# Two fused transformer layers on one Trainium2 core: the second feature projection by seven quadrant products, and another order for the end of the pass before it

## The reference

```python
xn = _rms_norm(x, norm_g[l]) * (1.0 + sc_x) + sh_x
fx_in, fx_gate, qx, kx, vx, nx_gate = _split_proj(xn @ w_in[l])
qx = _rms_norm(_heads(qx), q_norm_g[l])      # heads of 64
kx = _rms_norm(_heads(kx), k_norm_g[l])
```

## Time and profile before

| | us |
|---|---|
| median of 3 runs | 3401.26 (3400.95 to 3413.02) |
| the profiled execution, its own time | 3402.36 |
| its span (first to last instruction) | 3400.6 |
| second token pass, with the start of the feature pass | about 1845 to 2153 |
| second feature pass after its barrier | 2153.3 to 2693 |

### The profile page before, as it was taken

One profiled execution on the slowest core, in us unless ns is written; L12 is line 12 of the kernel. 1 busy time (PEld: TensorE's weight loads), 2 busy tenths in 40 slices (PEclk: granted clock), 3 DMA queues, 4 the chain that ended last, 5 costly groups with the idle time before them and its releaser, 6 DMA issues. The chain is left out here.

```text
span 3400.6 us, 39668 instructions
## 1 busy us (share of the span) xinstructions
PE 3111.9 (92%) x14503; PEld 2445.2 (72%) x14503; DVE 1514.0 (45%) x2504; ACT 941.8 (28%) x1520; POOL 795.5 (23%) x842
## 2 busy tenths in 40 slices
PE   3799999999988999775998999899999898999899
PEld 2588887888876666553897877677888675666687
DVE  6643333042306666386455222476000145777633
ACT  4422212110112334342222234322011133555400
POOL 5322222111112222265342222011111041000111
PEclk7899999999998999778898999999999998999999
DMA  7534335122243341314102666323211235776475
GB/s 272 184 97 116 102 101 180 61 77 75 75 127 87 90 105 55 90 47 97 43 26 82 200 185 208 109 112 123 74 74 74 99 102 134 155 158 142 112 199 148
DMA packets 325559, 390.82 MB, mean 115 GB/s; under 512 B 93879, under 2 KB 260264, under 8 KB 310696
## 3 DMA queue, kind: packets, MB, share of 16 engines
q1 hardware_dynamic: 320692, 387.11, 39.9%
q10 hardware_dynamic: 4704, 1.59, 0.2%
HBM read 256.77 MB, written 135.79 MB: 115 GB/s over the span
## 5 line engine op out<-in xcount | busy, mean ns | idle before, releaser
L691 PE MATMUL f_psum_out<-f_x_high,f_w_high 128*128 128x512 f32 (+1 forms) x1472 | 573.5, 390 | 18.8 <-DVE f_x_low L668 8.1
L691 PE MATMUL f_psum_out<-f_x_low,f_w_high 128*128 128x512 f32 (+1 forms) x1472 | 569.0, 387 | 0.0
L691 PE MATMUL f_psum_out<-f_x_high,f_w_low 128*128 128x512 f32 (+1 forms) x1472 | 568.6, 386 | 0.0
L691 PEld LDWEIGHTS f_psum_out<-f_x_high,f_w_high 128*128 128x128 f32 x1472 | 279.1, 190 | 77.9 <-issue 15.0
L691 PEld LDWEIGHTS f_psum_out<-f_x_low,f_w_high 128*128 128x128 f32 x1472 | 278.9, 189 | 56.5 <-issue 1.7
L691 PEld LDWEIGHTS f_psum_out<-f_x_high,f_w_low 128*128 128x128 f32 x1472 | 278.9, 189 | 55.5
L1351 PE MATMUL nbr_psum_o<-nbr_probT,nbr_v 128*128 128x512 f32 (+3 forms) x576 | 235.8, 490 | 0.0
L683 POOL CAST f_w_high<-f_w 128x1024 fp32r<-128x1024 f32 x41 | 42.6, 1040 | 747.8 <-PE f_psum_out L691 550.5
L532 PE MATMUL p_psum_proj<-p_w_high,p_h_high 128*128 128x512 f32 x512 | 207.5, 405 | 7.4 <-issue 4.0
L532 PE MATMUL p_psum_proj<-p_w_low,p_h_high 128*128 128x512 f32 x512 | 202.1, 395 | 0.0
L532 PE MATMUL p_psum_proj<-p_w_high,p_h_low 128*128 128x512 f32 x512 | 202.1, 395 | 0.0
(11 more groups left out here) (541 smaller groups left out, 6134.0 us busy)
## 6 DMA issues: line engine op xcount, KB each, us to landing
f_w<-in_w_fm SPq DMA_DIRECT2D x45, 512.0 KB, 5.7
side_ada_w<-in_w_ada_rows SPq DMA_DIRECT2D x24, 512.0 KB, 5.7
scratch_qkmT<-p_qkT_out SPq DMA_DIRECT2D x32, 384.0 KB, 4.6
scratch_z1T<-f_out SPq DMA_DIRECT2D x10, 1024.0 KB, 4.8
p_z<-scratch_z1T SPq DMA_DIRECT2D x16, 640.0 KB, 6.6
p_xt<-in_x SPq DMA_DIRECT2D x16, 512.0 KB, 3.9
p_staging<-in_w_tok SPq DMA_DIRECT2D x8, 1024.0 KB, 8.0
scratch_hT<-p_h_slot SPq DMA_DIRECT2D x16, 512.0 KB, 3.3
```

The lines of the kernel that those rows point to most:

```text
L691: last = nc.tensor.matmul(self.p_out[b][:, n * BANK + lo:n * BANK + hi], self.w_parts[b][w_part][:, k, :], self.x_parts[x_part][:, n, k, l ...
```

## The change

The product `W @ X` (output features by tokens) is cut into quadrants: W by pairs of output blocks and halves of the 1024 input features, X by halves of the input features and by even and odd tiles of 128 tokens. With sums of quadrants, seven quadrant products and some additions replace eight quadrant products. Everything below is one diff.

- `xn` is stored as `x2q`: the four quadrants of X (one of even or odd tiles each) and with them three sums and differences and a fourth, so 7 operands of [128, 4, 1024]; `combine` forms T1 to T4, by POOL for pairs 0 to 6 and by DVE for pair 7.
- The feature pass runs 24 items: 2 halves of the tokens by 12 pairs of blocks. An item is 7 products of 12 instructions each (4 slices, 3 parts), each into its own PSUM bank of six; DVE merges them. POOL adds weight quadrants and takes the rests, ACT rounds them, once for each item. The 7 input operands of a half stand in SBUF and are loaded again for the second half in item 11.
- The head norms take sums of 2 rows (2-column ones), which go to DRAM and come back spread over 128 partitions for root and reciprocal, go to DRAM again and come back broadcast.
- Results stand in three sets of rows (`SETS`), the third in the memory of the Fourier weights, which are loaded in item 20 instead of at the start.
- q and k items alternate with v and Fourier-input items (`F2_ORDER`). Loops of the pass are unrolled.
- In the token pass `before_pair` and `before_last` hold other work (`begin_next`, `go_on`), the last `turn_x` of tile 14 moves into the products of tile 15, and the last slot is filled by DVE.

```diff
+class QuadrantPass:
+    A11, A12, A22, S1, S2, S3, S4 = range(7)
+    B11, B21, B22, T1, T2, T3, T4 = range(7)
+    PRODUCTS = ((A11, B11), (S2, T2), (A12, B21), (S3, T3), (A22, T4), (S1, T1), (S4, B22))
+    N, HK, BANKS = 7, KB // 2, 6
+    def load_w(self, sp, n):
+        if n >= 2:
+            sp.wait_ge(self.a_ready, self.N * (n - 1))
+        sp.dma_start(<w[n % 2], two blocks, 1 MB>).then_inc(self.w_in[n % 2], 16)
+    def load_x(self, sp, half, i):
+        if half:
+            sp.wait_ge(self.prod_ready, self.N * (half * self.per_half - 1) + i + 1)
+        sp.dma_start(<x[i], 1 MB>).then_inc(self.x_in[i], 16)
+    def round_x(self, act, half, i):
+        act.wait_ge(self.x_in[i], 16 * (half + 1))
+        self.nc.scalar.activation(self.x[i][1][:], self.x[i][0][:], ACT.Copy).then_inc(self.x_rounded, 1)
+    def rest_of_x(self, eng, ops, half, i):
+        eng.wait_ge(self.x_rounded, self.N * half + i + 1)
+        ops.tensor_tensor(low, raw, high, ALU.subtract).then_inc(self.x_ready[i], 1)
+    def add_weights(self, pool, n):
+        pool.wait_ge(self.w_in[n % 2], 16 * (n // 2 + 1))
+        nc.gpsimd.tensor_tensor(s1, a21, a22, ALU.add)
+        nc.gpsimd.tensor_tensor(s3, a11, a21, ALU.subtract)
+        pool.drain()
+        nc.gpsimd.tensor_tensor(s2, s1, a11, ALU.subtract)
+        pool.drain()
+        nc.gpsimd.tensor_tensor(s4, a12, s2, ALU.subtract).then_inc(self.sums_ready, 1)
+    def round_w(self, act, n, i):        # waits prod_ready of item n-1, product i, and w_in or sums_ready
+    def rest_of_w(self, pool, n, i):     # waits a_rounded; tensor_tensor, 128x512
+    def product(self, pe, n, i):
+        pe.wait_ge(self.a_ready, self.N * n + i + 1)
+        if n % self.per_half == 0:
+            pe.wait_ge(self.x_ready[i], n // self.per_half + 1)
+        if self.N * n + i >= self.BANKS:
+            pe.wait_ge(self.prod_free, self.N * n + i + 1 - self.BANKS)
+        <12 matmuls of 128x512 into one bank>
 # tile_pass_2
+    def combine(eng, ops, j):
+        eng.wait_ge(combined_stored, 16 * (j + 1))
+        <4 tensor_tensor of 128x512, drains between>.then_inc(combined_ready, 1)
     def move(j, b):
         wait_apart(sp, x_filled, i + 1, taken)
-        sp.dma_start(cols_of(d["x2T"], i), slot[b][:])
+        <b == 0: slot[0] whole; b == 1: half of slot[1]>
+    def move_combined(j): <waits combined_ready, stores 1 MB>
     SP tile:
+        if b == 1 and not second and not last:
+            move_combined(j - 1)
         sp.wait_ge(x1_ready[b], j + 1)
-    next_weights (before_pair): fp.load(sp, d["w_fm2"], 0, b) for b in range(2)
-    begin_next (before_last):
-        sp.wait_ge(slices_used, 1)
-        fp.load_input(sp, d["x2T"], 0, 2)
-        sp.wait_ge(x1_ready[1], PAIRS)
-        fp.load_input(sp, d["x2T"], 2, 3)
+    begin_next (before_pair): fp.load_w(sp, 0); fp.load_x(sp, 0, 0)
+    go_on (before_last):
+        sp.wait_ge(mix_ready[1], PAIRS); sp.wait_ge(o_ready, NT - 1)
+        fp.load_x(sp, 0, 1)
+        move_combined(PAIRS - 2)
+        sp.wait_ge(slices_used, 1)
+        fp.load_x(sp, 0, 2); fp.load_x(sp, 0, 3)
+        sp.wait_ge(slices_used, 2)
+        fp.load_x(sp, 0, 4); fp.load_x(sp, 0, 5)
-    tiles(sp, tile, next_weights, begin_next)
+    tiles(sp, tile, begin_next, go_on)
+    sp.wait_ge(o_ready, NT); fp.load_x(sp, 0, 6); fp.load_w(sp, 1)
     move(PAIRS - 1, 1)
+    move_combined(PAIRS - 1)
 # PE after tile 15
-    fp.project_piece(nc, pe, 0, 0); turn_x(NT - 1); fp.project_piece(nc, pe, 0, 1)
-    pe.wait_ge(x_filled, NT); <pieces 0, 1 of block 1, piece 2 of both>
+    for i in range(fp.BANKS):
+        if i == 4:
+            pe.wait_ge(x_filled, NT)
+        fp.product(pe, 0, i)
+        if i == 1:
+            turn_x(NT - 1)
 # ACT
     fill: act.wait_ge(slot_stored[b], 16 * (j + 1))
+          act.wait_ge(combined_stored, 16 * (j + 1))
+    begin_next (before_pair): fp.round_x(act, 0, 0); fp.round_w(act, 0, i) for i in range(7)
+    go_on (before_last): fp.round_x(act, 0, 1); fill(PAIRS - 1, 0); fp.round_x(act, 0, 2); fp.round_x(act, 0, 3)
+    after the tiles: fp.round_x(act, 0, i) for i in range(4, 7)
 # POOL
+    tile, b == 0: wait_apart(pool, x_filled, 2 * j, taken); combine(pool, nc.gpsimd, j - 1)
+    begin_next: fp.add_weights(pool, 0); fp.rest_of_w(pool, 0, i) for i in range(3)
+    go_on: fp.rest_of_w(pool, 0, i) for i in range(3, 7);   at the end: fp.rest_of_x(pool, nc.gpsimd, 0, 5)
 # DVE
-    tiles(dve, tile, before_last=lambda: fp.rest_of_input(nc, dve, 0, 1))
+    begin_next (before_pair): fp.rest_of_x(dve, nc.vector, 0, 0)
+    go_on (before_last): fp.rest_of_x(dve, nc.vector, 0, 1);   in tile 15: rest_of_x 2
+    after the tiles: rest_of_x 3; <8 tensor_scalar fill slot[1]>; rest_of_x 4; combine(dve, nc.vector, PAIRS - 1); rest_of_x 6
+F2_ORDER = (0, 4, 1, 5, 2, 6, 3, 7, 8, 9, 10, 11)
 # feature_pass_2, one item n on each engine (kind: qk, v, in, gate)
+ SP:   load_w(n + 2); if n-1 is qk: spread_sums(n-1); store(n-1) if qk or v; n == 11: load_x(1, i) for 7 i;
+       n == 20: Fourier weights; store(n) if in or gate
+       spread_sums: rows -> rms_in (DRAM) -> spread [128,16] -> (root, reciprocal) -> rms_out (DRAM) -> work, broadcast to 64 partitions twice
+ PE:   product(n, i); after product 0 and 1 the sums of a qk item n-1 (two fp32 products each, ones[:, 0:P:HD]);
+       after product 1 and 3 the eight transposes each of a v item n-1
+ POOL: add_weights(n); rest_of_w(n, i) for 7 i
+ ACT:  round_w(n+1, i); empty sums or transposes of n-1; at i == 5: roots(n-1) and Square or Silu of n, b = 1; at the end b = 0
+ DVE:  merge(n, i): 8 operations of 128x512 an item, each frees a bank (prod_free); at i == 5 two reciprocals of 128x16;
+       after merge(n, 6): norm(n-1, 1), norm(n-1, 0), which wait for rms_in; n == 11: rest_of_x(1, i-3) after merges 3 to 6, then the last three
-    of_fourier loads at the start of the pass, Fori loops over pairs, RECIPROCAL of 128x2048
```

More of the change, by code:

```diff
@@ L2108, in _ @@
                 sp.sem_inc(slot_stored[b], 16)
+            sp.sem_inc(combined_stored, 16)
             load_x(0, 0)
@@ L2175, in tile @@
                     turn_y(j + 1, b)
-                if not first:
+                if not first and not (last and b == 1):
                     turn_x(2 * j + b - 1, first=second)
@@ L2212, in tile, with go_on @@
                     high(j + 1, b)
-                if not first:
+                if not first and not (last and b == 1):
                     fill(j + b - 1, 1 - b)
             def begin_next():
-                for b in range(2):
-                    fp.round_first_weights(nc, act, b)
-                fp.round_input(nc, act, 0, 2)
+                fp.round_x(act, 0, 0)
+                for i in range(fp.N):
+                    fp.round_w(act, 0, i)
+            def go_on():
+                fp.round_x(act, 0, 1)
+                fill(PAIRS - 1, 0)
+                fp.round_x(act, 0, 2)
+                fp.round_x(act, 0, 3)
             for k in range(MB):
@@ L2227, in _ @@
                 nc.scalar.activation(w_parts[0][:, k], staging[k % BUFFERS][:], ACT.Copy).then_inc(w_high_ready, 1)
-            tiles(act, tile, before_last=begin_next)
-            fill(PAIRS - 1, 1)
-            fp.round_input(nc, act, 2)
+            tiles(act, tile, begin_next, go_on)
+            for i in range(4, fp.N):
+                fp.round_x(act, 0, i)
         @block.gpsimd
@@ L2244, in tile, with go_on @@
                     low(j + 1, b)
+                if b == 0 and not first:
+                    wait_apart(pool, x_filled, 2 * j, taken)
+                    combine(pool, nc.gpsimd, j - 1)
             def begin_next():
-                for b in range(2):
-                    fp.rest_of_first_weights(nc, pool, b)
+                fp.add_weights(pool, 0)
+                for i in range(LOWS_FIRST):
+                    fp.rest_of_w(pool, 0, i)
+            def go_on():
+                for i in range(LOWS_FIRST, fp.N):
+                    fp.rest_of_w(pool, 0, i)
             low(0, 0, slice(LOW_FIRST, MB))
             low(0, 1)
-            tiles(pool, tile, before_last=begin_next)
+            tiles(pool, tile, begin_next, go_on)
+            fp.rest_of_x(pool, nc.gpsimd, 0, 5)
         @block.vector
@@ new lines, in _ @@
+            dve.wait_ge(slot_stored[1], 16 * PAIRS)
+            dve.wait_ge(combined_stored, 16 * PAIRS)
+            for k in range(KB):
+                nc.vector.tensor_scalar(slot[1][:, k, :], p_x[:, k, :], g.scale_x[:, k:k + 1], g.shift_x[:, k:k + 1], ALU.mult, ALU.add)
+            dve.drain().then_inc(x_filled, 1)
+            dve.wait_ge(x_filled, NT)
+            fp.rest_of_x(dve, nc.vector, 0, 4)
+            combine(dve, nc.vector, PAIRS - 1)
+            fp.rest_of_x(dve, nc.vector, 0, 6)
@@ L2375, in turn_v @@
-            def turn_v(j, b):
-                pe.wait_ge(vT_ready[b], j - FIRST_V + 1)
-                for n in range(NT):
```

(14 more changed lines are left out.)

497 lines of the change are left out of this document (344 added, 153 removed).

## The result

The changed kernel takes 3364.57 us (median of 4 runs, 3361.53 to 3367.08), the kernel before 3402.35 (4 runs, 3400.95 to 3413.02). The ratio is 0.9882, 95% interval 0.986 to 0.9904: faster by 1.2%. Forecast were 3343 us and a range of 3328 to 3372. The sign and the range held, the gain was 38 us where 59 were forecast, and the time lies 8.6 us outside the likeliest case's own range (3333 to 3356). The profiled execution took 3361.53 us with a span of 3359.8, so it stands against the 3344.4 of the sum: 17.1 us more.

A forecast was written before the change was run, and what follows sets the result against it. The feature pass was taken as bound by PE, the seam by loads, rounding and rests. From 3402.4, 61 us saved and 3 added gave 3344.4 for the profiled execution, 3343 as median; range 3328 to 3372.

The forecast's parts named there:

- 8, product (1, 0): New seam before the feature pass: tile 15 starts 9.2 us later, barrier 4.5 us earlier, item 1's first product at 2155.7.
- boundaries: Unrolled code and 161 product boundaries in the feature pass: 0 to 0.05 us each, 3 us added.
- part 7: Token pass: changed stores and the fill's wait cost +1 us over seven pairs, bounds -5 and +20.
- part 9: End of feature pass: shorter last silu and store take away about 1.2 of the 6.8 us wait.
- part 2: Merges and norms on DVE: norm 5.9 us, together 12 of an item's 19.1 us, hidden by PE.
- part 3: Norm's way through DRAM: DVE back 11.8 us into the item after, 16.3 allowed; priced at 0, cover 3.8 us.
- part 1: Feature pass: 2016 products instead of 2304 at 0.227 us save 65.4 us; sums and transposes unchanged at 34.8 us.
- rival C: Feature pass: each of 168 groups of 12 products loses 0.1 us or more, +17 us, 3360; chance 0.07.
- rival A: Norm's DRAM way is late by slow hops: 2.6 us for each of 8 qk items, 21 us, 3364; chance 0.12.
- rival D: POOL becomes the feature pass's bound, slower than before if a 128x512 operation takes 2.1 us; 3458 at 2.3; chance 0.04.
- part 6: Reloading the input operands in item 11: cover 2.7 us, loss of 2 us taken (0 to 6).
- Rival B: Token pass gets longer: fill waits 3 us for the combined store in seven pairs, +20, 3363; chance 0.12.

The follow-up runs named there:

- e7: Changed kernel with an item's first merge copy put ahead of the norm of two items earlier on VectorE: 3358.1 us, ratio 0.9866.
- e1: Changed kernel with GpSimd waiting for the norm's end of three items earlier before adding an item's weights: 3393.6 us, ratio 0.9977.
- e6: Changed kernel with 128 columns of ones instead of 2 as the sums' stationary operand: 3358.4 us, one run, no ratio.
- e8: Changed kernel with norm split around early merges, next pass's operands begun behind tile 14's work, and GpSimd's weight additions ahead of the barrier: 3353.3 us, ratio 0.9857.
- e9: e7's kernel with SyncE's weight loads moved ahead of the stores of the normed rows: 3351.2 us, ratio 0.9856.
- e10: Changed kernel with split norm, early weight loads, operands begun behind tile 14's work, and 128-column sums keeping heads apart: 3339.7 us, ratio 0.9828.
- e3: Changed kernel without the third set of rows, items taking two sets in turn: 3402.1 us, ratio 1.0012.

## Why the prediction was right or wrong

By its own steps, in the profiled execution (3361.5 against 3344.4):

| step | forecast | measured | to the sum |
|---|---|---|---|
| 1, products | 0.227 us each, 2016 | 0.22667 us, 2016 | -0.7 |
| 1, sums | 3.44 us an item | 4.07 | +5.1 |
| 1, transposes | 7.3 | 7.3 (1.82 an item; 20.86 us with them in e7, 19.04 without) | 0 |
| 2 and 3, norm | 5.9 us, hidden | 12.0; PE waits 9.9 in five items, 3.7 beside them | +13.6 |
| 6, refill | 2 | 3.5, with 0.9 of the waits on the copy | +1.5 |
| 8, product (1, 0) | 2155.7 | 2154.85 | -0.85 |
| slow clock in the pass's start | 1 | 1.7 | +0.7 |
| boundaries | +3 | 0 | -3 |
| end of the products to the end | 709.3 | 709.9 | +0.6 |

The forecast's 709.3 is 3344.4 less the 3 and the 2632.1 of its sum; it is the 709.4 of before with part 7's +1 and part 9's -1.2 in it. Whether part 9's 1.2 us came can't be told: from the last product to the end of the span the same code took 708.1 to 712.2 us from profile to profile. The 3.7 us beside the waits are products that start or run slowly behind them: about 1.5 of them in item 20, where after a wait of 3.17 us the granted clock is 0.60 from 2590 to 2594, and most of the rest at product 6 of the eight items behind a norm, at a clock of 1.00. The last column adds up to 17.0 of the 17.1 us.

**The step that failed** is part 2's "A norm ... 5.9 us ... hidden by PE", with the cover that part 3 built on it ("I price it at 0, with 3.8 us of cover"). The cover was about right. (The 34.3 of part 3 leaves the norm 5.3 us behind its loads, not 5.9, so its own numbers give 3.2 us of cover.) The DRAM way was done 28.6 us after the item's end where 29 had been said, and because the next item took 0.6 us longer by its sums, that was 5.5 us into the item after, not 6.5. With 12.0 us in the place of 5.9 the same working gives 5.5 + 12.0 + 0.7 - 16.3 = 1.9 us of wait, and 1.8 is what stands at 2286.35. The price had been taken from rows of a pass in which POOL was busy 14% of the time. The prediction did weigh the shared port, but put the norm's delay on POOL and DVE's only into the refill; in the norm it left DVE at its undisturbed rate. The Trainium skill, "SBUF — State Buffer", section "SBUF: two separate sides", says that whichever of the two engines starts first holds the pair of ports for its whole instruction and the other is blocked, so that either side can be the loser. By that rule the trace agrees in kind, and nearly in size: in the refill four rests on DVE took 12.47 us where four alone are 9.2, while POOL did a rest in 2.28 us and three additions in 3.14, 3.34 and 3.13 instead of 1.29. Three of these four ended within the 12.47 us; 9.2 + 3 x 1.29 = 13.1 would be all in turn, 0.6 more than measured. The merges stayed free of it, as said.

```profile
2396.63 12.47 DVE L783 TENSOR_TENSOR f_x_low<-f_x,f_x_high 128x2048 fp32r<-128x2048 f32 x4
```

```profile
2400.52 3.14 POOL L797 TENSOR_TENSOR f_sums<-f_w 128x512 f32<-128x512 f32 x1 [0.16 <-issue]
2403.62 3.34 POOL L798 TENSOR_TENSOR f_sums<-f_w 128x512 f32<-128x512 f32 x1
```

The time came to lie in the stated range only because that range had been widened for the rivals A to C, and its nearness to A's 3364 is luck: the waits have another cause.

**Right for the reasons given.** The saving in products (part 1, and rival C refuted: a boundary between groups of 12 costs nothing, 0.227 us as inside). The DMA hops (rival A refuted: PE's waits look like A's, on merges behind a norm, but the broadcast is in at 5.5 us; e1 makes the norm short, and the same waits vanish with the same hops). ACT hidden. POOL at 1.29 us where DVE leaves it alone, 1.48 and 1.60 us in the mean of the rests; rival D's 2.1 is reached only beside the norm and the rests. The seam's order of waits and their releasers. That product (1, 0) came within a microsecond of its 2155.7 was luck in part: tile 13's sum happened to come 2.6 us sooner than in the profile of before, while the wait before tile 15 was 11.2 us in place of 9.2 (the second one 4.2 in place of 4.3). From tile 13's sum the forecast had 75.2 us, the profile 77.0, seven profiles 78.0 in the mean.

**Sized wrong.** The sums: the text said that only the stationary side shrinks and that this changes nothing; it costs 0.54 of the 0.63 us an item (e6). The refill: 3.5 us, nearer to the 2 taken than to the 6 of the port's rule; DVE's last rest ended 18.6 us into item 12 (2409.10), where part 6 had 13.6, and the merge copy that product 6 needed stood behind it. The boundaries' 3 us were a surcharge without a row behind it. Of the signs named beforehand, "no wait of PE for DVE (prod_free) from item 1 on" is the one that failed.

**Not decided.** The token pass: -3.8 us in the first pair of profiles, -1.7 between the means of two of the kernel before and ten of the changed one, which is inside their spread, where the forecast had +1 with bounds -5 and +20. Rival B is refuted.

## What to carry to other kernels

A duration from a row holds for the company in which the row was taken: when a change makes GpSimd busy, price a group of VectorE's operations with two SBUF operands and casts at nearly twice its time (12.0 against 6.4 us here), and look at what stands behind them in VectorE's queue. What to do about it is not to make GpSimd wait (e1, 30 us lost) but to move what PE needs ahead of the slow group in the queue (e7, 9 us won in the pass), then to look at the next queue behind it (SyncE's loads, late in e8, early in e9 and e10). Buffers that seem a detail of the change can carry all of it: without its third set of rows the change gives nothing (e3).

## What the runs showed of the hardware

- VectorE beside GpSimd: 128x1024 operations of 1.28, 0.69 and 1.23 us take 1.95 to 2.22, 1.63 and 2.14; GpSimd's 128x512 of 1.29 take 1.7 to 2.3, beside a 128x2048 rest up to 3.4. With one operand in PSUM nothing changes (0.69).
- A stationary operand of 2 columns makes a group of fp32 products 0.27 us longer than one of 128 columns, though its load is shorter (0.085 against 0.188 us).
- Waits that return can cost the clock: in e1 (four waits of 7.3 to 8.5 us) and e3 (eight of 3.5 to 6.1) its mean over the pass was 0.96 and PE was busy 7.4 and 13.3 us longer for the same products; in e10, with 4.3 us of idle time, it was 1.00. In the changed kernel it stayed at 1.00 behind the waits of 1.8 us (2286 to 2290) and was 0.60 behind the one of 3.17 (2590 to 2594).
- The same code's token pass took 204.3 to 208.2 us, and began at 1864.8 to 1885.2, from profile to profile.
